# A feed-forward's first gate and value weights, split in the stage before it

## The chip, the cores and the metric

One NeuronCore of a Trainium2 chip. The time is the device's microseconds for one launch. TensorE multiplies matrices, VectorE and ScalarE do the elementwise work, GpSimd (POOL) small helpers and memsets, and the SP queue issues nearly all DMAs. All engines run by themselves and wait on semaphores.

## The reference

Two layers of a transformer trunk on 1024 tokens and 256 context tokens, width 1024. Each layer is a mixer (a convolution module and differential attention in layer 0, latent attention in layer 1), an output projection with norm, gate and residual, and a feed-forward. What matters here:

```python
def conv_ffn(h, w_up, conv_w, conv_b, w_down):
    u = h @ w_up
    val, gate = u[..., :FFN_HIDDEN], u[..., FFN_HIDDEN:]
    gate = depthwise_conv(gate, conv_w, conv_b)
    return (jax.nn.silu(gate) * val) @ w_down

x = x + mx[2] * rms_norm(yx, norm_mix_post[i])
hx = modulate(rms_norm(x, norm_ffn_pre[i]), mx[3], mx[4])
x = x + mx[5] * rms_norm(conv_ffn(hx, ...), norm_ffn_post[i])
```

`FFN_HIDDEN` is 2816, 22 tiles of 128. `w_up` is 1024 x 5632, the value half first.

## The kernel before

The kernel is a row of stages. Each has its own tiles in SBUF and its own semaphores; at its end the semaphores are cleared and all engines meet at a barrier (`stage`, L68, and `bare_stage`, L830; the barrier shows as L76). So no work of a stage begins before everything of the one before it is done.

**Exact products.** A float32 weight or activation is split into a rounded part, hi (type fp32r), and the rest, lo = raw - hi. `exact_product` (L84) takes three matmuls of 512 columns for one product: hi times hi, hi times lo, lo times hi (L88 to L90). Every weight must thus be loaded, rounded by ScalarE and subtracted by VectorE before TensorE may use it.

**The feed-forward** (`ffn`, L869; called twice: 10 token tiles in layer 0, 8 in layer 1). `raw`, `w_hi` and `w_lo` have four slots of 128 x 1024: value, gate and two for the down projection. One order of pieces, written by hand in `schedule`, is walked by every engine. It begins with the split of gate tile 0 (piece 0) and of value tile 0 (piece 1). A split is a 512 KB load on the SP queue (L977), a rounding on ScalarE (L1014) and a subtraction on VectorE (L1055) that raises `w_ready`. `product` on TensorE waits for `w_ready` at its piece and runs 8 x 3 matmuls for each chunk of up to 512 tokens. Behind piece 1 SP also loads the convolution's taps (L981, L983), and VectorE's `gate_work` waits for them, for the gate's chunks and for a memset of the sums by GpSimd (L1113). VectorE's first instruction in the stage is a memset of the gate tile (L1050), and bare increments follow it:

```python
dve.memset(gate[:, :], 0.0).then_inc(s.zeroed, 1)
dve.sem_inc(s.sum_done, SUMS)
```

**The join** (`join_project`, L1519) comes before the first feed-forward. It projects 10 token tiles with an output weight of 1024 x 1024, which it keeps split in `w_hi` and `w_lo` (8 slots of 1024 each). For tile t, behind TensorE's product: ScalarE copies and squares (L1747, L1753), GpSimd takes the inverse root (L1919, L1922), VectorE does the residual (L1859, L1863), ScalarE squares again (L1759), GpSimd takes a root, VectorE norms (L1868), TensorE turns (L1673), ScalarE modulates and rounds (L1769, L1774), VectorE subtracts (L1873). VectorE's order in loop step t is the residual of t-1, the norm of t-1, the rest of t-2. `work` has 8 slots of 1024: two for products, three for x, and others.

**The second output stage** (`project_out`, L1935) comes before the second feed-forward and does the same for 8 tiles with `TokenTail` (L246): VectorE runs `post_vector` of tile t (L344, L349), `pre_vector` of t-1 (L358, L362), `split_vector` of t-2 (L370, two halves). Its raw tile `y` has 8 slots; the weights' raw form lies in them at the start, and slots 0 and 1 take the products afterwards.

Of the kernel before, what the change touches and what calls it, by code (L numbers as in the profile page):

```python
# [11 lines left out]
ALU = mybir.AluOpType  # L12
# [856 lines left out]
def ffn(nc, name, tokens, h_hi, h_lo, y_sum, w_up, conv_w, conv_b, w_down, residual=None, following=None):  # L869
# [22 lines left out]
    with ExitStack() as ctx:  # L892
# [7 lines left out]
        w_hi = sb("w_hi", [P, 4, D], F32R)  # L900
        w_lo = sb("w_lo", [P, 4, D], F32R)
# [65 lines left out]
        def _(sp):  # L967
            def split(kind, tile, piece, back):
# [8 lines left out]
                sp.dma_start(raw[:, kind, :].rearrange("p (k n) -> p k n", n=src.shape[-1]), src)\  # L977
                  .then_inc(raw_in[kind], 16)
# [70 lines left out]
        def _(dve):  # L1049
# [3 lines left out]
            def split(kind, tile, piece, back):  # L1053
                dve.wait_ge(s.w_hi_done, piece + 1)
# [435 lines left out]
class OutWeights:  # L1490
# [3 lines left out]
    SIGNALS = ["w0_in", "w1_in", "w_hi_done", "w_ready"]  # L1494

    def __init__(self, nc, ctx, name, w_out, raw=None):
        self.w_out = w_out
        self.hi = ctx.enter_context(nc.sbuf_tensor(f"{name}_w_hi", [P, KD, D], F32R))
        self.lo = ctx.enter_context(nc.sbuf_tensor(f"{name}_w_lo", [P, KD, D], F32R))
        self.raw = raw if raw is not None else ctx.enter_context(nc.sbuf_tensor(f"{name}_raw", [P, 2, D], F32))  # L1500

    def load(self, sp, s, k):
        if k >= 2:

            sp.wait_ge(s.w_ready.sem, k - 1)
        sp.dma_start(self.raw[:, k % 2, :], self.w_out[k * P:(k + 1) * P, :])\
          .then_inc((s.w0_in, s.w1_in)[k % 2].sem, 16)

    def split_scalar(self, act, s, k):
        act.wait_ge((s.w0_in, s.w1_in)[k % 2].sem, 16 * (k // 2 + 1))  # L1510
        act.activation(self.hi[:, k, :], self.raw[:, k % 2, :], ACT.Copy).then_inc(s.w_hi_done.sem, 1)

    def split_vector(self, dve, s, k):
        dve.wait_ge(s.w_hi_done.sem, k + 1)
        dve.tensor_tensor(self.lo[:, k, :], self.raw[:, k % 2, :], self.hi[:, k, :].bitcast(F32), ALU.subtract)\
           .then_inc(s.w_ready.sem, 1)


def join_project(nc, y_hi, y_lo, conv_out, o_heads, ln_g, ln_b, subln, w_out, post, pre, x_old, x_new, ident):  # L1519
# [16 lines left out]
    with ExitStack() as ctx:  # L1536
        def sb(label, shape, dt=F32):
# [3 lines left out]
        w_hi, w_lo = (sb(f"w_{n}", [P, KD, D], F32R) for n in ("hi", "lo"))  # L1541
# [19 lines left out]
            "mean_full", "centred", "squared", "stat_full", "ms_done", "rstd_done", "spread", "normed", "silu_done",  # L1561
# [5 lines left out]
        block = ctx.enter_context(nc.Block())  # L1567

# [7 lines left out]
        def _(sp):  # L1576
# [56 lines left out]
        def _(pe):  # L1633
# [29 lines left out]
            def step(t, k, half):  # L1663
                cols_ = slice(half * BANK, (half + 1) * BANK)
                return exact_product(pe, ps[:, t % 2, cols_], y_hi[:, k, tokens(t)], y_lo[:, k, tokens(t)],
                                     w_hi[:, k, cols_], w_lo[:, k, cols_], k == 0, k == KD - 1)
# [47 lines left out]
        def _(act):  # L1714
            def weights(k):
                act.wait_ge(w_in[k].sem, 16)
                act.activation(w_hi[:, k, :], work[:, k, :], ACT.Copy).then_inc(s.w_hi_done.sem, 1)
# [82 lines left out]
        def _(dve):  # L1800
            def weights(k):
                dve.wait_ge(s.w_hi_done.sem, k + 1)
                dve.tensor_tensor(w_lo[:, k, :], work[:, k, :], w_hi[:, k, :].bitcast(F32), ALU.subtract)\
# [1320 lines left out]
```

## Time and profile before

| | us |
|---|---|
| median of 3 runs | 3630.87 |
| lowest and highest | 3623.41, 3631.25 |
| the profiled execution | 3627.79 |
| its span, first to last instruction | 3626.0 |
| TensorE busy | 3321.1 |
| VectorE busy | 1821.6 |
| ScalarE busy | 1169.1 |
| GpSimd busy | 294.6 |

The mean granted clock of TensorE was 0.956 of full speed. The execution's own time is 1.8 us over its span. Busy time is a mean over stages: in the feed-forwards TensorE is busy nearly all the time, at the stage boundaries no engine is. "<-" in a row names what released an engine from its idle time.

### The profile page before, as it was taken

Reading aid. Unit: us, or ns where it says so; the run is one execution under the profiler, and the core shown is the slowest. Engines: PE = TensorE matmul, PEld = TensorE weight load, DVE = VectorE, ACT = ScalarE, POOL = GpSimd, SP = SyncE. Lnnn points to the kernel's source line nnn. Section 1 sums busy time; section 2 is a strip of 40 time slices with the busy share of each in tenths; the row PEclk is TensorE's granted clock in tenths of the full one; section 3 lists DMA queues with packets and bytes.
Section 4 is the critical chain, followed back from the end, with each engine's and each line's share of the span. In section 5 each row is a group of like instructions: output and inputs, shape, how many; then the busy total and the mean of one; then the engine's idle time right before and its main releaser. Section 6 shows DMA issues by size and latency. Waiting matters only on the chain. (4 is left out here: it accounts for less than half of the span.)

```text
span 3626.0 us, 47627 instructions
## 1 busy us (share of the span) xinstructions
PE 3321.1 (92%) x18952; PEld 2782.4 (77%) x18952; DVE 1821.6 (50%) x2086; ACT 1169.1 (32%) x1913; POOL 294.6 (8%) x527
## 2 busy tenths in 40 slices
PE   3999599798999999999979698999999799999998
PEld 1787477676888888888869477888887688888886
DVE  4599666454344444444453334555554444444446
ACT  2212155456211111111146323555554322111121
POOL 1000000011000000000012111111111200000001
PEclk6999799889999999999989899999999899999999
DMA  5322587242211111111042743322212211111113
GB/s 182 83 83 97 160 276 240 102 127 76 63 50 40 35 35 35 35 40 41 30 135 83 260 167 97 103 51 53 60 40 76 73 62 48 51 46 58 35 47 116
DMA packets 277082, 316.29 MB, mean 87 GB/s; under 512 B 83825, under 2 KB 222673, under 8 KB 275905
## 3 DMA queue, kind: packets, MB, share of 16 engines
q1 hardware_dynamic: 264160, 267.09, 24.6%
q0 software_dynamic: 12768, 47.08, 3.5%
q8 instruction: 106, 1.74, 0.2%
q14 instruction: 48, 0.39, 0.0%
HBM read 243.54 MB, written 70.58 MB: 87 GB/s over the span
## 5 line engine op out<-in xcount | busy, mean ns | idle before, releaser
L1102 DVE TENSOR_TENSOR y_sum<-ffn_down_ps,y_sum 128x512 f32<-128x512 f32 x396 | 271.1, 690 | 238.2 <-PE ffn_down_ps L90 236.2
L88 PE MATMUL ffn_gate_ps<-y_hi,ffn_w_hi 128*128 128x512 f32 (+1 forms) x880 | 326.2, 371 | 22.6 <-DVE ffn_w_lo L1055 22.6
L88 PE MATMUL ffn_down_ps<-ffn_w_hi,ffn_act_hi 128*128 128x512 f32 x792 | 313.8, 396 | 16.8 <-DVE y_sum L1102 10.4
L89 PE MATMUL ffn_gate_ps<-y_lo,ffn_w_hi 128*128 128x512 f32 (+1 forms) x880 | 325.8, 370 | 0.0
L90 PE MATMUL ffn_gate_ps<-y_hi,ffn_w_lo 128*128 128x512 f32 (+1 forms) x880 | 325.6, 370 | 0.0
L89 PE MATMUL ffn_val_ps<-y_lo,ffn_w_hi 128*128 128x512 f32 (+1 forms) x880 | 323.9, 368 | 0.0
L88 PE MATMUL ffn_val_ps<-y_hi,ffn_w_hi 128*128 128x512 f32 (+1 forms) x880 | 323.8, 368 | 0.0
L90 PE MATMUL ffn_val_ps<-y_hi,ffn_w_lo 128*128 128x512 f32 (+1 forms) x880 | 323.7, 368 | 0.0
L89 PE MATMUL ffn_down_ps<-ffn_w_lo,ffn_act_hi 128*128 128x512 f32 x792 | 310.1, 392 | 0.0
L90 PE MATMUL ffn_down_ps<-ffn_w_hi,ffn_act_lo 128*128 128x512 f32 x792 | 309.8, 391 | 0.0
L1055 DVE TENSOR_TENSOR ffn_w_lo<-ffn_raw,ffn_w_hi 128x1024 fp32r<-128x1024 f32 x132 | 158.0, 1223 | 287.3 <-ACT ffn_w_hi L1014 287.3
L1035 ACT ACTIVATE ffn_act_hi<-ffn_conv 128x1024 fp32r<-128x1024 f32 x66 | 53.4, 841 | 593.3 <-DVE ffn_conv L1082 593.3
L2928 DVE TENSOR_REDUCE mla_neg_max<-mla_scores 128x1 f32<-128x1280 f32 x128 | 190.2, 1486 | 52.5 <-PE mla_scores L90 52.5
L1068 DVE TENSOR_SCALAR ffn_conv<-ffn_gate,ffn_taps 128x1281 f32<-128x1281 f32 (+1 forms) x44 | 38.8, 883 | 344.0 <-ACT ffn_gate L1024 344.0
L2842 PE MATMUL mla_turned<-ident,mla_e 128*128 128x128 f32 x1280 | 206.3, 275 | 1.9 <-ACT mla_pt L2906 1.3
L88 PEld LDWEIGHTS ffn_gate_ps<-y_hi,ffn_w_hi 128*128 128x128 f32 x880 | 167.2, 190 | 51.8 <-DVE ffn_w_lo L1055 23.4
L2898 ACT ACTIVATE mla_e<-mla_scores,mla_neg_max 128x1280 f32<-128x1280 f32 x128 | 170.0, 1328 | 111.6 <-DVE mla_neg_max L2928 111.6
L1014 ACT ACTIVATE ffn_w_hi<-ffn_raw 128x1024 fp32r<-128x1024 f32 x132 | 134.4, 1048 | 210.4 <-PE ffn_val_ps L90 195.5
L88 PEld LDWEIGHTS ffn_down_ps<-ffn_w_hi,ffn_act_hi 128*128 128x128 f32 x792 | 149.7, 189 | 59.2 <-DVE y_sum L1102 22.0
L2842 PEld LDWEIGHTS mla_turned<-ident,mla_e 128*128 128x128 f32 x1280 | 156.2, 141 | 48.0 <-issue 11.8
L666 DVE SCALAR_TENSOR_TENSOR ab_conv<-ab_u,ab_taps,ab_conv 128x1295 f32<-128x1295 f32 x120 | 188.1, 1567 | 3.2
L89 PEld LDWEIGHTS ffn_gate_ps<-y_lo,ffn_w_hi 128*128 128x128 f32 x880 | 167.2, 190 | 28.2
(293 smaller groups left out, 7022.9 us busy)
## 6 DMA issues: line engine op xcount, KB each, us to landing
ffn_raw<-in_ffn_w_up SPq DMA_DIRECT2D x88, 512.0 KB, 3.8
da_ada_w<-in_ada_w SPq DMA_DIRECT2D x10, 4096.0 KB, 24.5
ffn_raw<-in_ffn_w_down SPq DMA_DIRECT2D x44, 512.0 KB, 5.7
ab_raw<-in_ab_w_in SPq DMA_DIRECT2D x20, 512.0 KB, 3.8
mod_ada_w<-in_ada_w SPq DMA_DIRECT2D x4, 2048.0 KB, 11.1
scratch_mla_q_hi<-up_out_hi POOLq DMA_DIRECT2D x12, 512.0 KB, 2.9
scratch_mla_q_lo<-up_out_lo POOLq DMA_DIRECT2D x12, 512.0 KB, 3.2
scratch_qk_hi<-ab_qk_hi POOLq DMA_DIRECT2D x8, 640.0 KB, 3.2
```

Of the source, the lines that this page charges most:

```text
L88: pe.matmul(out, a_hi, b_hi, start=first, stop=False)
L89: pe.matmul(out, a_hi, b_lo, start=False, stop=False)
L90: return pe.matmul(out, a_lo, b_hi, start=False, stop=last)
L666: dve.scalar_tensor_tensor(out=out, in0=src[:, j:j + SPAN], scalar=taps[:, i, j:j + 1], in1=out, op0=ALU.mult, op1=ALU.add)\
L1014: act.activation(w_hi[:, kind, :], raw[:, kind, :], ACT.Copy).then_inc(s.w_hi_done, 1)
L1035: act.activation(act_hi[:, slot, b:b + m], conv[:, padded(b):padded(b) + m], ACT.Copy)\
L1055: dve.tensor_tensor(w_lo[:, kind, :], raw[:, kind, :], w_hi[:, kind, :].bitcast(F32), ALU.subtract).then_inc(s.w_ready, 1)
L1068: dve.tensor_scalar(inner, gate[:, 1:PAD - 1], here, bias, ALU.mult, ALU.add)\
L1102: dve.tensor_tensor(part, down_ps[:, half, :], part, ALU.add).then_inc(s.sum_done, 1)
L2842: mm = pe.transpose(t_ps[:, f % 2, m * P:(m + 1) * P], e[:, n % E_SLOTS, kt * P:(kt + 1) * P], ident[:, :])
L2898: act.activation(e[:, n % E_SLOTS, :], s_ps[:, n % 2, 0:T], ACT.Exp, bias=neg_max[:, n:n + 1], accum_out=sums[:, n:n + 1]).then_inc(s.exp. ...
L2928: dve.tensor_reduce(neg_max[:, n:n + 1], s_ps[:, n % 2, 0:T], AX.X, ALU.max, negate=True)\
```

## The change

The first gate tile and the first value tile of each feed-forward are loaded and split during the last tiles of the stage before it. The feed-forward's `w_hi` and `w_lo` become tiles that live across the boundary (`FirstWeights`, four slots each). While the output stage runs, these same tiles hold the upper half (k from 4 to 7) of that stage's own split weights (`Halves`); the lower half has tiles of its own. So the first split can be written only when TensorE has read the output weights for the last time, and VectorE waits for the last product (`y_full`). Both halves of the split, rounding and subtraction, are VectorE's now. In the feed-forward, pieces 0 and 1 are only increments.

```diff
+class FirstWeights:
+    SIGNALS = ["first0_in", "first1_in", "first_hi", "first_lo"]
+    KINDS = 1, 0
+    def __init__(self, nc, ctx, name, w_up, side):
+        self.hi, self.lo = (ctx.enter_context(nc.sbuf_tensor(f"{name}_first_{n}", [P, 4, D], F32R, side=side))
+                            for n in ("hi", "lo"))
+    def load(self, sp, n, raw, signal):
+        src = self.w_up.rearrange("(k p) (two f) -> p k two f", p=P, two=2)[:, :, self.KINDS[n], 0:P]
+        sp.dma_start(raw.rearrange("p (k n) -> p k n", n=P), src).then_inc(signal, 16)
+    def split(self, dve, n, raw, loaded, rounded, done):
+        kind = self.KINDS[n]
+        dve.wait_ge(loaded, 16)
+        dve.tensor_copy(self.hi[:, kind, :], raw).then_inc(rounded, 1)
+        dve.wait_ge(rounded, n + 1)
+        dve.tensor_tensor(self.lo[:, kind, :], raw, self.hi[:, kind, :].bitcast(F32), ALU.subtract).then_inc(done, 1)
+class Halves:
+    def at(self, k):
+        return self.lower[:, k, :] if k < KD // 2 else self.upper[:, k - KD // 2, :]
 def ffn(...)
-        w_hi = sb("w_hi", [P, 4, D], F32R)
-        w_lo = sb("w_lo", [P, 4, D], F32R)
+        w_hi, w_lo = first.hi, first.lo
   SP, split:
-                if not (isinstance(piece, int) and piece < 2):
+                if isinstance(piece, int) and piece < 2:
+                    sp.sem_inc(raw_in[kind], 16)
+                else:
                     sp.wait_ge(s.w_ready, piece - (back - 1))
...
   ScalarE, split:
+                if isinstance(piece, int) and piece < 2:
+                    act.sem_inc(s.w_hi_done, 1)
+                    return
   VectorE, split:
+                if isinstance(piece, int) and piece < 2:
+                    dve.sem_inc(s.w_ready, 1)
+                    return
 def join_project(...)
+        first_raw = [work[:, X + (N - 3) % 3, :], work[:, N % 2, :]]
   SP:
                 inputs(t + 2)
+                if t == N - 1:
+                    sp.wait_ge(x_stored[(N - 3) % 3].sem, 16 * ((N - 3) // 3 + 1))
+                    sp.wait_ge(s.h_done.sem, N - 2)
+                    first.load(sp, 0, first_raw[0], first_in[0])
                 store_x(t - 1)
+                if t == N - 1:
+                    first.load(sp, 1, first_raw[1], first_in[1])
   VectorE:
+                if t == N:
+                    dve.wait_ge(s.y_full.sem, N)
+                    first.split(dve, 0, first_raw[0], first_in[0], s.first_hi.sem, s.first_lo.sem)
                 if 1 <= t < N + 1:
                     residual(t - 1)
+                if t == N:
+                    first.split(dve, 1, first_raw[1], first_in[1], s.first_hi.sem, s.first_lo.sem)
 def project_out(...)
+        first, first_raw = weights.first, [y[:, 2, :], y[:, 3, :]]
   SP:
+                if t == N - 4:
+                    sp.wait_ge(s.w_ready.sem, KD)
+                    for n in range(2):
+                        first.load(sp, n, first_raw[n], first_in[n])
   VectorE:
+                if t == N - 1:
+                    dve.wait_ge(s.y_full.sem, N)
+                    first.split(dve, 0, first_raw[0], first_in[0], s.first_hi.sem, s.first_lo.sem)
                 if t < N:
                     tail.post_vector(dve, t, t, y[:, t % 2, :])
+                if t == N - 1:
+                    first.split(dve, 1, first_raw[1], first_in[1], s.first_hi.sem, s.first_lo.sem)
                 if 1 <= t < N + 1:
                     tail.pre_vector(dve, t - 1, t - 1)
```

Every use of the output weights changes from `w_hi[:, k, :]` to `w_hi.at(k)`, and likewise for lo.

## Rows read from the trace of the kernel before

**Rows 1.** The page, busy time, share of the span and instructions of each engine.

```profile
PE 3321.1 (92%) x18952; PEld 2782.4 (77%) x18952; DVE 1821.6 (50%) x2086; ACT 1169.1 (32%) x1913; POOL 294.6 (8%) x527
```

**Rows 2.** The chain that ended last, in order of time: start, duration, what.

```profile
2869.89 5.05 DMA ffn_raw<-in_ffn_w_up
...
2877.33 0.79 PE ffn_gate_ps L88
```

**Rows 3.** Timeline, first feed-forward's start: start us, duration us, engine, line, operation, [idle before].

```profile
903.25 1.22 DVE L1873 TENSOR_TENSOR y_lo<-out_work,y_hi 128x1024 fp32r<-128x1024 f32 x1 [4.12 <-ACT y_hi L1774]
...
905.50 8.63 POOL L1113 MEMSET y_sum<- 128x10240 f32 x1 [10.60 <-POOLq L76]
...
905.84 1.13 DVE L1050 MEMSET ffn_gate<- 128x1283 f32 x1 [1.36 <-PEq L76]
...
911.83 0.79 PE L88 MATMUL ffn_gate_ps<-y_hi,ffn_w_hi 128*128 128x512 f32 x1 [12.97 <-DVE ffn_w_lo L1055]
```

**Rows 4.** Timeline of VectorE, second feed-forward's start.

```profile
2868.36 0.69 DVE L370 TENSOR_TENSOR y_lo<-out_turned,y_hi 128x512 fp32r<-128x512 f32 x1 [0.16 <-ACT y_hi L406]
2870.17 0.91 DVE L1050 MEMSET ffn_gate<- 128x1026 f32 x1 [1.11 <-PEq L76]
```

**Rows 5.** Timeline of TensorE, first matmul of the latent attention.

```profile
2213.97 0.77 PE L88 MATMUL mla_scores<-k_first_hi,q_first_hi 96*128 96x512 f32 x1 [11.06 <-PEq L76]
```

**Rows 6.** Timeline of TensorE, where matmuls become short in each feed-forward.

```profile
917.12 0.42 PE L88 MATMUL ffn_gate_ps<-y_hi,ffn_w_hi 128*128 128x512 f32 x1
...
2883.04 0.49 PE L89 MATMUL ffn_gate_ps<-y_lo,ffn_w_hi 128*128 128x512 f32 x1
```

**Rows 7.** Groups of VectorE instructions, by form: count, busy us, mean ns, idle before.

```profile
L2936 DVE COPY mla_pt<-mla_turned 128x512 f32<-128x512 f32 x128 | 87.8, 686 | 131.7 <-PE mla_turned L2842 131.7
...
L1868 DVE TENSOR_SCALAR out_work<-out_work,out_small 128x1024 f32<-128x1024 f32 x10 | 7.5, 746 | 5.3 <-POOL out_small L1922 5.3
```

**Rows 8.** Timeline, the join's last tiles, VectorE, GpSimd and TensorE.

```profile
886.14 1.23 DVE L1873 TENSOR_TENSOR y_lo<-out_work,y_hi 128x1024 fp32r<-128x1024 f32 x1 [2.22 <-ACT y_hi L1774]
...
889.41 0.19 POOL L1919 TENSOR_SCALAR out_small<-out_small 128x1 f32<-128x1 f32 x1 [6.27 <-ACT out_work L1753]
889.68 0.55 POOL L1922 TENSOR_TENSOR out_small<-out_small,out_minus_half 128x1 f32<-128x1 f32 x1
...
890.26 1.28 DVE L1859 SCALAR_TENSOR_TENSOR out_work<-out_work,out_small,out_gates 128x1024 f32<-128x1024 f32 x1 [2.89 <-POOL out_small L1922]
...
894.93 0.75 DVE L1868 TENSOR_SCALAR out_work<-out_work,out_small 128x1024 f32<-128x1024 f32 x1 [2.13 <-POOL out_small L1922]
...
896.92 1.94 PE L1673 MATMUL out_turned<-ident,out_work 128*128 128x128 f32 x8 [8.97 <-ACT out_work L1769]
```

**Rows 9.** Timeline, the second output stage's last tiles.

```profile
2854.98 0.19 POOL L419 TENSOR_SCALAR out_small<-out_small 128x1 f32<-128x1 f32 x1 [7.97 <-ACT out_junk L389]
...
2857.15 1.22 DVE L349 TENSOR_TENSOR out_x<-out_x,out_raw 128x1024 f32<-128x1024 f32 x1
...
2857.25 1.53 POOL L421 TENSOR_TENSOR out_small<-out_small,out_minus_half 128x1 f32<-128x1 f32 x1
...
2858.82 1.28 DVE L358 SCALAR_TENSOR_TENSOR out_h<-out_x,out_small,out_rows 128x1024 f32<-128x1024 f32 x1 [0.44 <-POOL out_small L421]
```

**Rows 10.** The page, DMA issues: count, KB each, median us to landing.

```profile
ffn_raw<-in_ffn_w_up SPq DMA_DIRECT2D x88, 512.0 KB, 3.8
```

**Rows 11.** The taps in the first feed-forward: issue, landing, first use.

```profile
912.92 1.66 SPq L983 DMA_DIRECT2D ffn_taps<-in_ffn_conv_b  x1
...
ffn_taps<-in_ffn_conv_b SPq DMA_DIRECT2D x1, 11.0 KB, 5.1
...
928.80 0.95 DVE L1068 TENSOR_SCALAR ffn_conv<-ffn_gate,ffn_taps 128x1281 f32<-128x1281 f32 x1 [14.87 <-ACT ffn_gate L1024]
```

**Rows 12.** Timeline of TensorE, behind the first feed-forward's loop.

```profile
1802.48 0.77 PE L88 MATMUL ffn_down_ps<-ffn_w_hi,ffn_act_hi 128*128 128x512 f32 x1 [3.24 <-issue]
```

More of the change, by code:

```diff
@@ L866, in split_vector, with __init__, ffn @@
                           ALU.subtract).then_inc(s.next_ready, 1)
-def ffn(nc, name, tokens, h_hi, h_lo, y_sum, w_up, conv_w, conv_b, w_down, residual=None, following=None):
+class FirstWeights:
[4 more added lines that the diff above has]
+                            for n in ("hi", "lo"))
+        self.w_up = w_up
+    def load(self, sp, n, raw, signal):
[8 more added lines that the diff above has]
+class Halves:
+    def __init__(self, lower, upper):
+        self.lower, self.upper = lower, upper
+    def at(self, k):
+        return self.lower[:, k, :] if k < KD // 2 else self.upper[:, k - KD // 2, :]
+def ffn(nc, name, tokens, h_hi, h_lo, y_sum, w_up, conv_w, conv_b, w_down, first, residual=None, following=None):
     chunks = token_chunks(tokens)
@@ L972, in split @@
                     src = w_down[bass.ds(tile * P, P), :].rearrange("(k p) n -> p k n", k=1)
-                if not (isinstance(piece, int) and piece < 2):
+                if isinstance(piece, int) and piece < 2:
+                    sp.sem_inc(raw_in[kind], 16)
+                else:
                     sp.wait_ge(s.w_ready, piece - (back - 1))
                     sp.sem_inc(s.asked, 1)
-                sp.dma_start(raw[:, kind, :].rearrange("p (k n) -> p k n", n=src.shape[-1]), src)\
-                  .then_inc(raw_in[kind], 16)
+                    sp.dma_start(raw[:, kind, :].rearrange("p (k n) -> p k n", n=src.shape[-1]), src)\
+                      .then_inc(raw_in[kind], 16)
                 if isinstance(piece, int) and piece == 1:
@@ L1490, with __init__, join_project @@
 class OutWeights:
[L1494 to L1519, printed above, removed]
+    def __init__(self, nc, ctx, name, w_out, raw, first):
+        self.w_out, self.raw, self.first = w_out, raw, first
+        self.hi, self.lo = (Halves(ctx.enter_context(nc.sbuf_tensor(f"{name}_w_{n}", [P, KD // 2, D], F32R)), upper)
+                            for n, upper in (("hi", first.hi), ("lo", first.lo)))
+def join_project(nc, y_hi, y_lo, conv_out, o_heads, ln_g, ln_b, subln, w_out, post, pre, x_old, x_new, ident, first):
     AT = A_WIDTH // P
@@ L1540, in join_project @@
         work = sb("work", [P, 8, D])
-        w_hi, w_lo = (sb(f"w_{n}", [P, KD, D], F32R) for n in ("hi", "lo"))
+        w_hi, w_lo = (Halves(sb(f"w_{n}", [P, KD // 2, D], F32R), upper)
+                      for n, upper in (("hi", first.hi), ("lo", first.lo)))
         uo = sb("uo", [P, 2, KD, P])
@@ L1567, in join_project @@
         block = ctx.enter_context(nc.Block())
+        first_raw = [work[:, X + (N - 3) % 3, :], work[:, N % 2, :]]
+        first_in = [s.first0_in.sem, s.first1_in.sem]
         def tokens(t):
@@ L1942, in project_out @@
         ps = ctx.enter_context(nc.psum_tensor(f"{name}_ps", [P, 2, D], F32))
-        s = ctx.enter_context(stage(nc, name, TokenTail.SIGNALS + ["y_full", "y_copied", "w_hi_done", "w_ready"]))
+        s = ctx.enter_context(stage(nc, name, TokenTail.SIGNALS + ["y_full", "y_copied", "w_hi_done", "w_ready"]
+                                    + FirstWeights.SIGNALS))
+        first, first_raw = weights.first, [y[:, 2, :], y[:, 3, :]]
+        first_in = [s.first0_in.sem, s.first1_in.sem]
         tail = TokenTail(nc, ctx, name, s, post, pre, 2 if tokens > SEQ else 1, N, ident)
@@ L3077, in trunk @@
                 first_head.close()
-                weights = OutWeights(nc, projection, "out1", i.c_w_out[0], w_raw)
+                first = FirstWeights(nc, layer1, "ffn1", i.ffn_w_up[1], "right")
+                weights = OutWeights(nc, projection, "out1", i.c_w_out[0], w_raw, first)
                 project_out(nc, "out1", y_hi, y_lo, SEQ, weights, (mods(1, MIX_GATE, 1), i.norm_mix_post[1]),
@@ L3083, in trunk @@
                 ffn(nc, "ffn1", SEQ, y_hi, y_lo, y_sum, i.ffn_w_up[1], i.ffn_conv_w[1], i.ffn_conv_b[1],
-                    i.ffn_w_down[1], ((mods(1, FFN_GATE, 1), i.norm_ffn_post[1]), tile_of(x3), tile_of(out)))
+                    i.ffn_w_down[1], first, ((mods(1, FFN_GATE, 1), i.norm_ffn_post[1]), tile_of(x3), tile_of(out)))
 def rope_constants():
```

23 lines of the change are left out of this document (13 added, 10 removed).

## The prediction

> **What bounds the kernel now.** I read the page's busy times first: TensorE is busy for 3321.1 of 3626.0 us [rows 1], so only what makes TensorE wait, or runs it at its lower clock, is worth anything. Then the chain that ended last, in order of time: it runs through the second feed-forward and begins with that stage's first weights, a DMA at 2869.89, ScalarE's rounding, VectorE's subtraction and TensorE's first matmul at 2877.33 [rows 2]. That is 7.44 us in which nothing but these weights is on its way. Last, the timeline at both stage boundaries. In the first feed-forward the join's last operation ends at 904.47 (903.25 + 1.22), GpSimd starts the next stage at 905.50, VectorE its memset at 905.84, and TensorE gets its first weights at 911.83 after 12.97 us of idling [rows 3]. In the second the end of the stage before is 2869.05 (2868.36 + 0.69), VectorE starts at 2870.17 [rows 4] and TensorE at 2877.33 [rows 2]. From each first matmul on, TensorE sets the time, so an earlier start moves the rest by as much.
>
> **What the change removes.** At each feed-forward's start: two loads of 512 KB, two roundings, two subtractions; the engines raise the semaphores instead. TensorE then waits for one thing, VectorE's increment of w_ready, which stands in VectorE's queue behind the memset of the gate tile. Two bounds. If the increment goes as soon as the memset is under way, TensorE starts a little after 905.84. If it goes only when the memset has ended, TensorE starts just after 906.97 (905.84 + 1.13). The kernel has no row for such a bare increment with an engine waiting for it. But where a bare increment must follow an operation (lines 2624 and 2625), the code puts a wait before it, so I take the earlier side, with some time for the semaphore: 906.25. The first feed-forward gains 911.83 - 906.25 = 5.6 us (4.8 at the other bound, 5.9 at most). TensorE can start this soon after a boundary: the latent attention, which waits for nothing, has its first matmul at 2213.97 straight behind the barrier [rows 5].
>
> **The clock.** TensorE starts each feed-forward at the lower level (1.2 GHz): its matmuls of 512 columns become short (0.42 us and less) only at 917.12, 5.3 us after the start, and in the second at 2883.04, 5.7 us after it [rows 6]. The last turn of the join, at 896.92, already takes 1.94 us for 8 small matmuls [rows 8] and is followed by a pause either way. The shorter pause (7.4 us instead of 13.0) gives me no reason for a warm start, so this cold piece moves and stays. It costs nothing here; for the range, half a cold piece more or less is about 1.3 us each (half of 5.3, at half speed).
>
> **What it adds: a copy and a subtraction on VectorE, twice per boundary.** The subtraction has the form of the one at 903.25, 1.22 us [rows 3]. A VectorE copy from SBUF to SBUF of 1024 is not in the trace. Below it stands the one-source operation of that size, 0.75 us (L1868); above, the copy of 512 from PSUM takes 0.69 us, so 1024 at that rate is under 1.4 us [rows 7]. It has one source in SBUF, like L1868, so I take 0.75; with 0.04 between, one split is 2.02 us, at most 2.65.
> The Trainium skill (VectorE: DVE Perf Modes, section on the perf-mode tier table) puts an fp32 tensor_copy and tensor_scalar in SBUF in one class at double rate; by that rule it is 0.75 too. I have no run of the copy.
>
> **First boundary, gate split.** It sits behind the wait for the last product and before the residual of tile 9. TensorE's last product ends at 886.92 (896.92 less 8.97 idle less the 1.03 of the turn behind it); VectorE is free at 887.37 (886.14 + 1.23). So the split runs 887.40 to 889.42 (to 890.05 at most). GpSimd starts the root at 889.41 and VectorE takes it up at 890.26 [rows 8]: the idle time covers the split. What it can cost is the delay of GpSimd's operation, 0 to 0.7 us; I take 0.1. A delay here is on the path, since the residual feeds ScalarE, which does tile 8's modulation next.
> **Value split.** Behind the residual, 892.85 to 894.87. The norm of tile 9 stood at 894.93, released by GpSimd [rows 8], whose two steps now fall beside the subtraction. The second stage shows what that does: GpSimd's root takes 0.55 us alone [rows 8], but 1.53 (2857.25 to 2858.78) beside a VectorE addition that ends at 2858.37 [rows 9]. So the norm starts at about 895.6 and ends at 896.35. The turn that reads it starts at 896.92, and waits for ScalarE [rows 8]: 0.5 us to spare, cost nothing; with the slow copy the spare is used up and up to 0.3 us shows.
> The Trainium skill (GPSIMD Engine Reference, Specifications) says GpSimd shares its SBUF interfaces with VectorE when VectorE reads two SBUF inputs or runs in a 2-port mode. This speaks against both splits, whose copy is in the second class and subtraction in the first; the sum by it is the one just made, since the 1.53 us row already has it.
>
> **Second boundary, gate split.** In the first stage GpSimd's root started 2.5 us behind the product's end, so here (2854.98) the product ends near 2852.5 and the split is over near 2854.6: covered, 0 to 0.6 us, and I take 0.
> **Value split.** Here there is no cover. VectorE ends the residual at 2858.37, waits 0.45 us, and from 2858.82 works almost without a pause through tiles 6 and 7: each one's scaling, shift and the subtractions between [rows 9]; the turns and roundings follow these. The split of 2.02 and its gap go in at 2858.40, so 2858.82 becomes 2860.47. All behind it goes 1.65 us later, and so does the stage's end (2.3 at most by the slow copy; 0.4 more if GpSimd's root of 2857.25 has to wait out the split as well). TensorE starts the second feed-forward at 2870.17 + 1.65 + 0.4 = 2872.2. It gains 2877.33 - 2872.2 = 5.1 us. With the increment behind the memset (0.91) it gains 4.55.
>
> **Queues.** In SP's queue of the join the gate load waits for tile 7's store and norm, both older than the store of tile 8 behind it, so nothing is held up. Each raw tile is queued a product ahead of its split; such a load lands in 3.8 us [rows 10]. In the feed-forward the taps' four small loads are now first in SP's queue. The last was issued at 912.92 and landed 5.1 us later, at 918.0; they come 1.06 us sooner, so at 917.0. VectorE needed them at 928.80 and will at 923.2 [rows 11]: 6 us to spare, and in the second stage some 3. GpSimd's memset of the sums, also awaited there, ends at 914.13 (905.50 + 8.63) [rows 3]. Later tiles' loads and TensorE's loop are untouched.
>
> **The sum.** 5.6 - 0.1 + 5.1 = 10.6 us. The profiled execution took 3627.79 us (span 3626.0), which gives 3617.2. The shown median, 3630.87, is 3.1 higher, the lowest run 4.4 lower; all four executions average 3628.3, less 10.6 is 3617.7. I say 3618.
>
> **Rivals.**
> (a) The increment waits for the memset and the copy is slow: 4.8 - 0.8 + 4.55 - 0.65 = 7.9 us, 3620. For it: both bounds above are open. Against: the copy has the shape of L1868. This is the weak end of the same case.
> (b) TensorE's instructions are not there at the boundary. After the loop, at 1802.48, it sat idle for 3.24 us with nothing that the trace shows to wait for [rows 12]. If that came behind each barrier, TensorE would start near 908.8 (905.5 + 3.24) and 2874.8: 3.0 + 2.5 - 0.1 = 5.4 us, 3623. Against: rows 5, and both boundaries are straight code.
> (c) Slower. A second wait, now hidden behind the weights, ends at 911.83 and 7 us behind the second barrier (the same 3.24 twice over, or a late barrier), so no start is gained. The value split's 1.65 to 2.7 us on the second boundary and the gate split's 0.1 to 0.7 remain: 1.8 to 3.4 us slower, 3630 to 3631. It decides once that hidden wait ends later than 6.3 us behind the barrier. Against: TensorE followed VectorE's subtraction at once in both places.
> (d) The clock comes back sooner in the second stage, since the turns lie only 3 us ahead of the first product: up to 2.8 us more gain, 3615. For it: the shorter pause. Against: the turns there run cold and are few.
>
> **Chances.** Forecast with (a) as its end 0.78, (b) 0.07, (c) 0.04, (d) 0.11. The range adds the clock's 1.3 us twice, (a), and the runs' own scatter of about 4 us either way: 3612 to 3625. A change under 0.2% (7.3 us) can't be told from none here. By the median shown, faster means below 3623.6. I give faster 0.80, within 0.2% 0.17, slower 0.03.
>
> **What would show it.** First matmul of the first feed-forward near 906.3 and 5.4 us after it the fast matmuls. In the join, the residual of tile 9 at 890.3 or 890.4, the norm near 895.6, the last subtraction still at 903.3. In the second stage tile 6's scaling 1.65 us later than now against the residual before it, and the stage's end as much. No VectorE wait on the taps. The copy at 0.75 us. I am wrong if TensorE idles over 2 us behind a barrier, if the turn at 896.92 moves by more than 0.5 us, or if the second boundary's gain is under 4.

## The result, and the profile after

The changed kernel takes 3636.18 us (median of 20 runs, 3627.09 to 3643.13), the kernel before, on the same chip, 3625.23 (median of 20 runs, 3618.03 to 3634.78): ratio 1.0028, 95% interval 1.0022 to 1.0035. It is slower by 0.3%, where I had forecast 3618 and 0.3% faster, and it lies outside my range of 3612 to 3625.

The profiled execution took 3635.7 us, its span is 3633.9 and the mean granted clock 0.958 (before: 3627.79, 3626.0, 0.956). So the clock is no cause of the loss. The page's busy times, to be held against [rows 1]:

```profile
PE 3343.7 (92%) x18952; PEld 2783.4 (77%) x18952; DVE 1824.0 (50%) x2090; ACT 1164.2 (32%) x1909; POOL 294.8 (8%) x527
```

TensorE executes the same 18952 matmuls and is busy for 22.6 us more. VectorE has the 4 operations more and ScalarE the 4 fewer that the diff says. So I looked for the lost time inside TensorE's own work, not in a wait.

Both boundaries, on the other hand, did what was forecast. The timeline of the changed kernel (columns as in [rows 3]), first the join's last tiles and the first feed-forward's start, then the second output stage's and the second feed-forward's start:

```profile
886.40 0.69 DVE L888 CAST ffn_first_hi<-out_work 128x1024 fp32r<-128x1024 f32 x1
887.12 1.23 DVE L890 TENSOR_TENSOR ffn_first_lo<-out_work,ffn_first_hi 128x1024 fp32r<-128x1024 f32 x1
888.54 0.19 POOL L1957 TENSOR_SCALAR out_small<-out_small 128x1 f32<-128x1 f32 x1 [6.28 <-ACT out_work L1786]
...
889.39 1.28 DVE L1892 SCALAR_TENSOR_TENSOR out_work<-out_work,out_small,out_gates 128x1024 f32<-128x1024 f32 x1 [1.04 <-POOL out_small L1960]
...
892.57 1.23 DVE L890 TENSOR_TENSOR ffn_first_lo<-out_work,ffn_first_hi 128x1024 fp32r<-128x1024 f32 x1
893.21 0.64 POOL L1957 TENSOR_SCALAR out_small<-out_small 128x1 f32<-128x1 f32 x1 [3.85 <-ACT out_work L1792]
...
894.51 0.75 DVE L1901 TENSOR_SCALAR out_work<-out_work,out_small 128x1024 f32<-128x1024 f32 x1 [0.71 <-POOL out_small L1960]
...
902.37 1.23 DVE L1906 TENSOR_TENSOR y_lo<-out_work,y_hi 128x1024 fp32r<-128x1024 f32 x1 [4.11 <-ACT y_hi L1807]
904.65 8.64 POOL L1153 MEMSET y_sum<- 128x10240 f32 x1 [10.17 <-POOLq L76]
...
904.87 0.80 PE L88 MATMUL ffn_gate_ps<-y_hi,ffn_first_hi 128*128 128x512 f32 x1 [6.88 <-DVEq L1092]
904.99 1.13 DVE L1087 MEMSET ffn_gate<- 128x1283 f32 x1 [1.39 <-PEq L76]
...
2849.24 1.23 DVE L349 TENSOR_TENSOR out_x<-out_x,out_raw 128x1024 f32<-128x1024 f32 x1
2849.34 1.76 POOL L421 TENSOR_TENSOR out_small<-out_small,out_minus_half 128x1 f32<-128x1 f32 x1
2850.39 0.68 DVE L888 CAST ffn_first_hi<-out_raw 128x1024 fp32r<-128x1024 f32 x1
...
2852.25 1.28 DVE L358 SCALAR_TENSOR_TENSOR out_h<-out_x,out_small,out_rows 128x1024 f32<-128x1024 f32 x1
...
2861.78 0.69 DVE L370 TENSOR_TENSOR y_lo<-out_turned,y_hi 128x512 fp32r<-128x512 f32 x1 [0.16 <-ACT y_hi L406]
...
2863.56 0.79 PE L88 MATMUL ffn_gate_ps<-y_hi,ffn_first_hi 128*128 128x512 f32 x1 [2.44 <-DVEq L1092]
2863.62 0.91 DVE L1087 MEMSET ffn_gate<- 128x1026 f32 x1 [1.14 <-PEq L76]
```

This trace runs 0.88 us ahead of the one before already at the join's last tiles (902.37 against 903.25 [rows 3]). At the first boundary TensorE starts 1.27 us behind the end of the stage (903.60 to 904.87), where it started 7.36 behind it. At the second it starts 1.09 us behind (2862.47 to 2863.56), where it was 8.28. The second feed-forward starts at 2863.56 instead of 2877.33, 13.8 us sooner, and yet the span ends 7.9 us later. So its 748.7 us have become 770.3.

That stage can be read off one row. ScalarE rounds each of the 22 hidden tiles once, just behind TensorE's products for it. The view of that tile's instructions (count, shortest, median and longest in ns, start of the first and of the last), second feed-forward, kernel before:

```profile
L1035 ACT ACTIVATE ffn_act_hi<-ffn_conv x22: 1056/1061/1064, 2905.8 to 3584.3; 128x1024 fp32r<-128x1024 f32 x22
```

the first feed-forward (44 instructions) in the kernel before and in the changed one, and the changed kernel's second:

```profile
L1035 ACT ACTIVATE ffn_act_hi<-ffn_conv x44: 397/729/1062, 946.1 to 1800.7; 128x1024 fp32r<-128x1024 f32 x22, 128x256 fp32r<-128x256 f32 x22
...
L1072 ACT ACTIVATE ffn_act_hi<-ffn_conv x44: 397/729/1062, 938.8 to 1793.4; 128x1024 fp32r<-128x1024 f32 x22, 128x256 fp32r<-128x256 f32 x22
...
L1072 ACT ACTIVATE ffn_act_hi<-ffn_conv x22: 1056/1060/1062, 2892.3 to 3590.9; 128x1024 fp32r<-128x1024 f32 x22
```

From first to last tile the second feed-forward takes 698.6 us instead of 678.5. The first takes 854.6, and 854.6 before. Below I call this the tile time. The distance from one 512-column matmul's start to the next (mean over some 250 to 400 neighbours, in windows spread over the stage), which I call the step, tells the same:

```
step, ns                     gate    value   down   | output stage ahead
before, 1st feed-forward     226.9   227.3   227.3  | 228.8
before, 2nd                  226.7   226.6   227.4  | 227.1
changed, 1st                 226.9   227.3   227.3  | 228.8
changed, 2nd                 234.2   234.3   233.4  | 232.2
```

The granted clock is 1.00 in both kernels from 2910 to 3560 us. The second feed-forward has 3168 such matmuls, and 3168 at 7 ns more are 22 us: that is the loss. What differs between the two feed-forwards is where the diff put their tiles. The tiles' addresses, which no trace shows, are, in bytes along a partition: before, w_hi and w_lo of the second at 100992 and 117376; changed, first_lo at 196576 and first_hi at 212960, since they were allocated on the right side of the memory, which is filled from 229344 downwards. The first feed-forward's went to 100992 and 117376. I give addresses by what is left over a multiple of 256: y_hi, y_lo and the activations stand at 128 in both kernels, so do all feed-forward weights of before and the changed kernel's first ring (the four slots of first_hi and first_lo), but the second ring stands at 224.

### The profile page after: what moved, and what is told of

Same layout as the page of the kernel before. It is cut to its first block and busy times, and to the rows that moved or that the text cites. A ratio compares the mean times of both kernels' runs of the same rounds, so it can differ in the third digit from the quotient of the medians.

```text
span 3633.9 us, 47642 instructions
## 1 busy us (share of the span) xinstructions
PE 3343.7 (92%) x18952; PEld 2783.4 (77%) x18952; DVE 1824.0 (50%) x2090; ACT 1164.2 (32%) x1909; POOL 294.8 (8%) x527
## 3 DMA queue, kind: packets, MB, share of 16 engines
q1 hardware_dynamic: 264160, 267.09, 24.6%
## 5 line engine op out<-in xcount | busy, mean ns | idle before, releaser
L88 PE MATMUL ffn_gate_ps<-y_hi,ffn_first_hi 128*128 128x512 f32 (+1 forms) x880 | 328.6, 373 | 9.3 <-DVEq L1092 9.3
L88 PE MATMUL ffn_down_ps<-ffn_first_hi,ffn_act_hi 128*128 128x512 f32 x792 | 315.2, 398 | 15.7 <-DVE y_sum L1142 9.2
L89 PE MATMUL ffn_gate_ps<-y_lo,ffn_first_hi 128*128 128x512 f32 (+1 forms) x880 | 328.2, 373 | 0.0
L90 PE MATMUL ffn_gate_ps<-y_hi,ffn_first_lo 128*128 128x512 f32 (+1 forms) x880 | 327.9, 373 | 0.0
L89 PE MATMUL ffn_val_ps<-y_lo,ffn_first_hi 128*128 128x512 f32 (+1 forms) x880 | 326.7, 371 | 0.0
L88 PE MATMUL ffn_val_ps<-y_hi,ffn_first_hi 128*128 128x512 f32 (+1 forms) x880 | 326.5, 371 | 0.0
L90 PE MATMUL ffn_val_ps<-y_hi,ffn_first_lo 128*128 128x512 f32 (+1 forms) x880 | 326.3, 371 | 0.0
L90 PE MATMUL ffn_down_ps<-ffn_first_hi,ffn_act_lo 128*128 128x512 f32 x792 | 311.7, 394 | 0.0
L89 PE MATMUL ffn_down_ps<-ffn_first_lo,ffn_act_hi 128*128 128x512 f32 x792 | 311.0, 393 | 0.0
L88 PEld LDWEIGHTS ffn_gate_ps<-y_hi,ffn_first_hi 128*128 128x128 f32 x880 | 167.4, 190 | 40.7 <-DVEq L1092 10.1
L88 PEld LDWEIGHTS ffn_down_ps<-ffn_first_hi,ffn_act_hi 128*128 128x128 f32 x792 | 149.4, 189 | 59.5 <-DVE y_sum L1142 20.9
L89 PEld LDWEIGHTS ffn_gate_ps<-y_lo,ffn_first_hi 128*128 128x128 f32 x880 | 167.3, 190 | 30.4
L90 PEld LDWEIGHTS ffn_gate_ps<-y_hi,ffn_first_lo 128*128 128x128 f32 x880 | 167.2, 190 | 30.5
```

Of the source, the lines that this page charges most:

```text
L88: pe.matmul(out, a_hi, b_hi, start=first, stop=False)
L89: pe.matmul(out, a_hi, b_lo, start=False, stop=False)
L90: return pe.matmul(out, a_lo, b_hi, start=False, stop=last)
```

## The experiments

My theory from here on: the start address of a matmul's operand costs TensorE time. Rivals: the ring as such (two stages sharing tiles, the upper half used by the output stage), or the loads and splits that are missing at the stage's start. For each run I give the time and, as ratio or difference, how it stands to the kernel before on the same chip; where there is a single run, I say so and go by its trace.

**Ring moved by 32 bytes (e1), weights of before moved by 32 bytes and its activations by 64 (e2), only the first boundary changed (e3), second boundary with the gate weights alone (e4).**

```
e1: + layer1.enter_context(nc.sbuf_tensor("pad1", [P, 8], F32, side="right"))
      first = FirstWeights(nc, layer1, "ffn1", i.ffn_w_up[1], "right")
e2: + if name == "ffn1": sb("pad_a", [P, 8])      # ahead of w_hi
    + if name == "ffn1": sb("pad_b", [P, 8])      # behind w_lo
e3: - first = FirstWeights(nc, layer1, "ffn1", i.ffn_w_up[1], "right")
    + first = None       # output weights and the stage's start as before
e4: e1, and
    + EARLY = 1 if name == "ffn1" else 2          # pieces that are split ahead
    - first.split(dve, 1, first_raw[1], ...)      # value split of project_out
```

> The kernel after, with 32 bytes of padding on the right side of SBUF ahead of the second feed-forward's early weights, so that they begin at multiples of 64 bytes (196544 and 212928 instead of 196576 and 212960). Theory A (a matrix operand that begins 32 bytes past a multiple of 64 makes every matmul step slower): the chunks of the second feed-forward come back from 5.62 to 5.44 us, the output stage's tile from 12.02 to 11.79, and the kernel is about 22 + 2 us faster than the kernel after, so some 14 to 16 us faster than the kernel before (ratio 0.996). Theory B (the weights lie too far up in SBUF, beside the sums): no change by 32 bytes, ratio stays 1.003. Theory C (something else in the second stage's new order): also 1.003.

> The kernel before, with 32 bytes of padding ahead of the second feed-forward's w_hi and w_lo and 32 bytes behind them; only these two tiles move (101024 and 117408 instead of 100992 and 117376), nothing of the early split is in it. Theory A: chunks of 5.62 us in the second feed-forward alone, about 22 us slower, ratio 1.006. Theories B and C: as before, ratio 1.000.

> The early split at the first boundary only; the second output stage and feed-forward as in the kernel before. All theories: the first boundary's gain alone, about 6.4 us (ratio 0.998), and no slow chunks in the second feed-forward. If the first boundary's gain were lost later, the ratio would be 1.000.

> The padded kernel, and at the second boundary only the gate tile is split early; the value tile is loaded, rounded and subtracted inside the feed-forward as before, beside the gate product. Expected if the value split's 1.3 us on VectorE's path is what the output stage's end gained in length: 1.3 us less than the padded kernel, TensorE's first value product not delayed. With theory A true the ratio to the kernel before is 0.995 to 0.996; with B or C 1.002 to 1.003.

Measured: e1 3627.01 us, 1.0008 (0.9999 to 1.0017), steps 233.3, 233.2 and, down, 229.0: a multiple of 64 gave back only part, so neither of my forecasts for e1 (0.996 or 1.003) came. e2 3641.69 us, 1.0051 (1.0037 to 1.0065), steps 233.3 in all three. e3 3616.32 us, 0.9979 (0.9969 to 0.9988), steps 227. e4 3625.89 us, 1.0004 (0.9995 to 1.0013), steps as e1.

e2 is the decisive one: the kernel before, with its stages untouched and some tiles of its second feed-forward further up, loses nearly what the changed kernel loses there. The two pads move more than its expectation says: the weights go from 128 to 160 over a multiple of 256, and the activations, which lie behind both pads, to 192. Its tile time is 697.0 us:

```profile
L1039 ACT ACTIVATE ffn_act_hi<-ffn_conv x22: 1056/1060/1062, 2901.0 to 3598.0; 128x1024 fp32r<-128x1024 f32 x22
```

So the loss comes without the ring and with all splits in their old place; e8 and e16 below show the other side, a ring without the loss. e3 shows the first boundary's gain alone. e4 shows no gain from the value split at the second boundary: the stage's end comes 1.3 us sooner without it (10.68 us behind the residual, 12.01 in e1), and e4 and e1 can't be told apart in time.

**Other operands, other distances (e5, e6, e7), ring moved by 96 bytes (e8).**

```
e5: kernel before; pads of 8 floats ahead of y_hi1 and of act_hi (second
    feed-forward), weights not to be moved off their multiples of 128
e6: w_hi, w_lo = (sb(n, [P, 4 * D + 32], F32R)[:, at:at + 4 * D]...)
    # at = 4 floats in the first feed-forward, 12 in the second
e7: the same with at = 24 and 16
e8: e1 with [P, 24] in place of [P, 8]
```

> The kernel before, with the other matmul operands of the second output stage and feed-forward moved: y_hi1 and y_lo1 begin at 19104 and 51872 (32 past a multiple of 128), the two act tiles likewise; the weights stay at multiples of 128. So the gate and value products have a shifted moving operand only, the down product and the output product a shifted stationary one only. Steps so far (start to start, 512 columns): 227 ns with all tiles at multiples of 128; 233.3 with the weights at 32 past, in either role. Theory A1 (the start of either operand counts, whichever tile it is): 233 ns in all three products and in the output product. Theory A2 (it is something of the weight tiles alone): 227.

> The kernel before, with w_hi and w_lo of the first feed-forward beginning 16 bytes past a multiple of 128, and of the second 48 past. Theory A (every start off the grid costs the same): 233 ns in both feed-forwards. If only multiples of 32 other than 0 cost: 227 in the first. If the cost grows with the offset, the second is slower than the first.

> The kernel before, with w_hi and w_lo of the first feed-forward beginning 96 bytes past a multiple of 128 and of the second 64 past, low in SBUF. The kernel after had 96 past and lay high: 234.2 ns for gate and value (weights stationary), 233.4 for down (weights moving). The padded one had 64 past and lay high: 233.3 and 229.0. Theory A with a grid of 128 bytes: the same pairs here, 234.2 and 233.4 in the first feed-forward, 233.3 and 229.0 in the second. Theory B2 (a grid of 64, and the high place costs the rest): 233 in the first, 227 and 227 in the second.

> The kernel after, with 96 bytes of padding in place of 32 ahead of the second feed-forward's early weights: they begin at 196480 and 212864, multiples of 128, as high up as before. Grid of 128: 227 ns in every product, the kernel some 14 us faster than before (ratio 0.996). Theory B2 (the high place): 233 and 229 as in the first padded kernel, ratio 1.001.

Measured: e5 3643.07 us, a single run, steps 234.3 (gate, value), 233.3 (down), 233.4 (output). e6 3649.46, a single run, first feed-forward 234.3, 234.5 and 231.3, second 230.1, 229.8 and 232.0. e7 3658.09, a single run, first 233.0, 232.9 and 233.3, second 231.7, 231.9 and 230.5. e8 3609.37 us, 0.9958 (0.9944 to 0.9971), all steps of the second feed-forward 226.6 to 227.0.

e8 gives back all of it, and beats both kernels. From these runs I concluded that every operand had to start on a multiple of 128. That was wrong, and two slips hid it: in e5 the pads took the weights from 128 to 0 over a multiple of 256 (y to 160, the activations to 32), and in e6 and e7 the tiles had grown by 128 bytes, so that w_lo stood 128 off w_hi. The steps of e6 and e7 fit none of the rules written down for them.

**All other matmul tiles on multiples of 128 (e9), the same with the gate weights alone (e10), and 128 bytes or one tile alone (e11).**

```
e9:  e8, its 96 bytes now at the top of the right side (the latent
     attention's q and k move too), + sb("pad", [P, 24]) ahead of lat_h_hi
e10: e9, and e4's edit
e11: kernel before; at = 32, 32 floats (w_hi, w_lo) in the first
     feed-forward, 0, 8 in the second, in tiles that grew by 128 bytes
```

> The kernel after with 96 bytes of padding at the top of SBUF's right side, once, so that every tile on that side begins at a multiple of 128 (the second feed-forward's early weights at 196480 and 212864, and the latent attention's first head's q and k too, which were 96 past in the kernel before), and 96 bytes ahead of the latents stage's h_hi and h_lo, which were 32 past in the kernel before. Theory: the ratio of the kernel padded to 128 (0.996) and, if the latents' moving tiles paid as the weights did, up to 240 x 3 matmuls x 5 ns = 3.6 us more, about 0.995. If short matmuls and another bound hide it there: 0.996.

> The kernel with all tiles on the grid of 128, and the value split of the second boundary left in the feed-forward. The value split lengthened VectorE's path from the last residual to the stage's end from 10.68 to 12.01 us; here 10.68, so 1.3 us less than the kernel with all on the grid; below what the rounds can tell (0.1%), so the trace decides.

> The kernel before, with w_hi and w_lo of the first feed-forward 128 bytes further on (multiples of 256, where every fast case so far was 128 past one), and in the second only w_lo moved, to 32 past a multiple of 128. If the grid is 128: 227 ns in the first feed-forward. If it matters which half of 256 a tile begins in: slower. If each instruction pays for its own operand: in the second feed-forward one matmul in three (the one that reads w_lo) pays 6.5 ns, a mean of 229; if one shifted tile slows the whole row: 233.

Measured: e9 3609.5 us, 0.9960 (0.9946 to 0.9974), e10 3608.46, 0.9961 (0.9948 to 0.9975): nothing more to gain there, and again no difference by the value split. e11 3648.45 us, a single run, 24.6 over the kernel before: in the first feed-forward the gate and value steps are 233.1 and 233.2, down 228.9, although every tile starts on a multiple of 128. (w_hi stood at 0 over a multiple of 256 and w_lo, for the grown tile, at 128.) In the second, where w_lo came to 32 over a multiple of 256, they are 233.3, 233.4 and, down, 231.8. My rule fell. Nearly all tiles of the kernel before stand at 128 over a multiple of 256, so place by itself and place against the other operand had never been told apart.

**Everything moved alike (e12, e13), one operand by 128 bytes, one tile by 32 (e14, e15).**

```
e12: + sb("pad_all", [P, 8])     # ahead of the first tile: all 32 bytes up
e13: + sb("pad_all", [P, 32])    # all 128 bytes up
e14: w tiles grown by 256 bytes; first: both at 32 floats; second: 0 and 8
e15: the same; first: act tiles at 32 floats, w at 0; second: w_hi 8, w_lo 0
```

> The kernel before with one pad of 32 bytes ahead of its first tile, so that nearly every tile of it (weights, hidden rows, activations, alike) starts 32 bytes further up and all stand as before to each other: all at 160 over a multiple of 256, where before all stood at 128. Nothing else changes. Theory A (what counts is where an operand starts by itself, and the good place is the one that all tiles of before share): both feed-forwards and the output stages step 6 to 8 ns longer per 512-column product (227 to 233 or more), some 6700 of them in the two feed-forwards and more elsewhere, so the time is 45 to 60 us over the kernel before. Theory B (what counts is how the stationary and the moving operand of one product stand to each other): every step stays at 226.6 to 227.4 ns and the time stays within 3 us of the kernel before.

> The kernel before with a pad of 128 bytes ahead of its first tile: nearly all tiles start at a multiple of 256 where before they stood 128 over one. Theory A with a grid of 128 bytes: no change, steps of 227 ns. Theory A with a grid of 256 (which the last look suggests, where the first feed-forward's w_hi stood at a multiple of 256 and stepped 233 ns): steps of 233 ns, time 45 us up or more. Theory B: steps of 227 ns and the time of the kernel before, within 3 us.

> The kernel before with the feed-forwards' weights in views of larger tiles. First feed-forward: w_hi and w_lo both start 128 bytes further up (multiples of 256), the hidden rows and activations stay at 128 over one. Second: w_hi stays, w_lo alone starts 32 bytes further up. A grid of 128: the first feed-forward stays at 227 ns. A grid of 256, by itself or between the two operands: 230 to 234 ns in gate, value and down products. If only the relation of hi to lo counts, the first stays at 227 ns, since both moved alike. Second: if a shifted tile costs only the products that read it, the value and gate steps rise by a third of the full 7 ns (one product of three reads w_lo), to 229 ns; if one shifted tile disturbs its neighbours in the order too, to 233 ns as with both shifted.

> The kernel before with weights and activations of the feed-forwards in views of larger tiles. First feed-forward: activations start 128 bytes further up (a multiple of 256), weights stay: gate and value products stay at 227 ns by every theory (if they don't, the distance of the tiles w_hi and w_lo, now 16640 bytes instead of 16384, counts), and the down products, with act stationary at 0 and weights moving at 128 over a multiple of 256, stay at 227 ns with a grid of 128 and go to 229 to 234 ns with one of 256. Second: w_hi alone starts 32 bytes further up: two of three products read it, so 231 to 232 ns if only those pay, 233 ns or more if the third pays too.

Measured, a single run each, kernel before 3627.06: e12 3628.57 and e13 3627.09, every step within 0.3 ns of before. e14 3665.18: first feed-forward 232.6, 232.4 and 232.3, second 233.5, 233.4 and 232.3. e15 3651.11: first 227.2, 227.4 and down 232.2, second 231.8, 231.8 and 232.5. The tile times of the second feed-forward, e12:

```profile
L1035 ACT ACTIVATE ffn_act_hi<-ffn_conv x22: 1056/1061/1064, 2905.2 to 3583.7; 128x1024 fp32r<-128x1024 f32 x22
```

678.5 us to the tenth as before, with nearly all tiles at 160, where e2 had the weights at 160, y at 128 and the activations at 192 and paid 18.5 us. So 160 is not a bad place by itself, nor is 128 needed (e13 has nearly all at 0); what counts is how the two operands of a product stand to each other. e14's first feed-forward (871.2 us of tile time against 854.6) shows that 128 bytes between them cost, too. In e15's first, w_lo stands 256 bytes further from y than in before, and gate and value are at 227: 256 cost nothing.

**The changed kernel's ring left where it is, the rest brought to it (e16).**

```
e16: changed kernel, + sb("pad_all", [P, 24])   # left side 96 bytes up: to 224
```

> The changed kernel with its ring of first weights left where it is (196576 and 212960, 224 over a multiple of 256), and one pad of 96 bytes ahead of the first tile on the left side, so that hidden rows, y, the output stages' lower halves and the activations come to 224 over a multiple of 256 too. By the relation of the two operands (what the last four looks showed for the kernel before) the second feed-forward steps at 227 ns again, the last output stage too, and the time is that of the version with the ring moved: 0.9945 to 0.9970 of the kernel before. By a place that is good or bad in itself, it keeps the 234 ns in the second feed-forward: 1.002 to 1.004, or worse still where the first one joins it.

Measured: 3610.88 us, 0.9967 (0.9952 to 0.9981), steps 226.7, 226.7 and 227.1, output stage 227.1, and the tile time 678.3:

```profile
L1072 ACT ACTIVATE ffn_act_hi<-ffn_conv x22: 1056/1062/1064, 2890.6 to 3568.9; 128x1024 fp32r<-128x1024 f32 x22
```

The ring is at 196576 and 212960 as in the changed kernel, and the loss is gone. The feed-forward products in which hi and lo stood alike, and e5's output stage, by the stationary operand's start less the moving one's, modulo 256:

```
difference   step, ns         where
  0          226.6 to 227.4   before, e8, e9, e10, e12, e13, e16
 32          233.3            e2 gate, value, down; e5 down
 64          233.2, 233.3     e1 gate, value
 96          234.2 to 234.3   changed kernel and e5, gate and value
128          232.2 to 232.6   e14 first feed-forward; e15 first, down
160          233.4            changed kernel, down; e5 output stage
192          229.0            e1 down
```

**One tile alone: where the cost falls.** In e14's second feed-forward only w_lo is off. The timeline of TensorE there, matmuls and, last, the weight load (PEld) of an L90:

```profile
3000.07 0.40 PE L88 MATMUL ffn_gate_ps<-y_hi,ffn_w_hi 128*128 128x512 f32 x1
3000.31 0.40 PE L89 MATMUL ffn_gate_ps<-y_lo,ffn_w_hi 128*128 128x512 f32 x1
3000.55 0.39 PE L90 MATMUL ffn_gate_ps<-y_hi,ffn_w_lo 128*128 128x512 f32 x1
3000.78 0.40 PE L88 MATMUL ffn_gate_ps<-y_hi,ffn_w_hi 128*128 128x512 f32 x1
...
3000.31 0.19 PEld L90 LDWEIGHTS ffn_gate_ps<-y_hi,ffn_w_lo 128*128 128x128 f32 x1
```

The product with w_lo is L90. Over the some 700 gate and value steps of each line in that stage, the one that begins with L89 is the long one, 239.0 ns; the one that begins with L90 itself is 228.3, and L88's 232.6 (before: 226.6 to 226.8). While L89 streams y_lo, the weights of L90 are being loaded. So most of the cost falls in the product during which the misplaced tile is loaded, and little in the one that multiplies by it. It is not all of it: L88's step neither reads nor loads w_lo and is 5.9 ns longer too. In e15's second feed-forward, with w_hi alone off, all three are longer: L88 231.7, L89 230.8 (during which w_lo, in its old place, is loaded), L90 233.1. The loads' own mean stays at 187 to 188 ns in every kernel, so the trace shows the moving operand delayed, not the load. That the two reads collide in the memory is my reading of this; no run shows it directly, and a collision of these two reads alone doesn't explain L88's step.

## Why the prediction was wrong

**The step that failed** is "Later tiles' loads and TensorE's loop are untouched", and with it "From each first matmul on, TensorE sets the time, so an earlier start moves the rest by as much". The diff moves the loop's weights to other addresses, and I never asked what that does to 3168 matmuls. It held because of a premise at the very start, "only what makes TensorE wait, or runs it at its lower clock, is worth anything": TensorE's rate at full clock was taken as fixed, and it is not. The misplaced operands cost 21.7 us in the second feed-forward and about 1.8 in the output stage ahead of it, whose upper weight halves are the same tiles (its tiles' turns are 12.02 us apart, 11.79 before). None of my rivals had it; my slower one, (c), was a hidden wait, and no such wait appeared. None of the signs of being wrong that I had named came either (TensorE starts 1.3 and 1.1 us behind the two stages' ends, the turn of 896.92 keeps its place, the second boundary gains 5.9 us): they all looked at the boundaries, and the loss was in the stage behind.

**The rest held.** With the two operands brought together the kernel takes 3609.37 us (e8), 13.9 under the kernel before on its chip, where I had 10.6; e9, e10 and e16 are 14.3, 15.4 and 12.8 under theirs. The interval of e8 is 10.5 to 20.3 us, so my sum was at its low end. Part of the rest is the clock, as shown below, and not a better start.

- First boundary: 6.1 us from the earlier start, 5.6 forecast. The bare increment didn't wait for the memset: TensorE's matmul at 904.87 is earlier than the memset's start at 904.99. The cold piece, up to the first short matmul, is 4.4 us (904.87 to 909.31) instead of 5.3 (917.12 less 911.83 [rows 3, 6]), so the gain is 6.4 by the first hidden tile (938.8 against 946.1, less the 0.9 of lead).
- Copy: 0.69 us, 0.75 forecast; subtraction 1.23.
- Gate split in the join: GpSimd starts at 888.54, which is 889.41 [rows 8] less the 0.88 by which this trace is ahead, and the residual at 889.39, 890.26 [rows 8] less the same: cost nothing, 0.1 forecast.
- Value split there: GpSimd's first step took 0.64 us instead of 0.19 beside the subtraction, and the norm came at 894.51, 0.46 us late against 894.93 [rows 8] (0.7 forecast). The last subtraction kept its place: 902.37. The Trainium skill (GPSIMD Engine Reference, Specifications) names two-input VectorE instructions as contenders for the interfaces that GpSimd shares; these rows agree.
- Second boundary: the value split costs 1.32 us (12.00 from the residual's end to the stage's, 10.68 before [rows 4, 9]), 1.65 forecast. The 0.45 us in which VectorE waited for GpSimd vanished into it, though GpSimd's root stretched to 1.76 us. TensorE's start against the residual's end gained 5.9 us (18.96 [rows 2, 9] to 13.09), 5.1 forecast.
- Rival (d), a warmer start, came in small: cold pieces of 4.4 us and, in the second (2863.56 to 2868.42), 4.9, for 5.3 and 5.7. It is not one number: at the first boundary the traces have 4.0 to 5.7 us where the weights are loaded behind the barrier, and 3.2 to 4.9 where they are ready. Rival (b)'s 3.24 us [rows 12] did not come behind the barriers.
- Taps: no VectorE wait on them; its first operation on the gate, at 921.51, was released by ScalarE.

The account by the two traces: 0.9 us ahead at the join, 6.4 at the first boundary, 5.9 at the second, and 0.6 in between (some 2.4 gained, less the output stage's 1.8) make the 13.8 us by which the second feed-forward starts sooner; its own 21.7 turn them into 7.9 lost. The 2.4 are the clock's. Behind the first feed-forward's loop TensorE pauses in both kernels, for 3.24 us [rows 12] and 3.25. Then the kernel before executes 12 matmuls at the lower level, 0.63 us or more each, and the changed kernel none; first the kernel before, then the changed one:

```profile
1803.05 0.63 PE L89 MATMUL ffn_down_ps<-ffn_w_lo,ffn_act_hi 128*128 128x512 f32 x1
...
1795.17 0.47 PE L88 MATMUL ffn_down_ps<-ffn_first_hi,ffn_act_hi 128*128 128x512 f32 x1 [3.25 <-issue]
1795.48 0.39 PE L89 MATMUL ffn_down_ps<-ffn_first_lo,ffn_act_hi 128*128 128x512 f32 x1
```

The lead grows from 7.3 us ahead of these matmuls to 9.8 behind them, and what the clock gives and takes in the stages after that nearly cancels. I don't count this as a gain of the early split: e7, which splits at the old place, has no such slow matmuls either, and e8, which splits early, has 8.

## What to carry to other kernels

When a change moves a tile that TensorE reads, note the start address, and compare stationary and moving operand modulo 256 bytes: a pad of 24 floats (96 bytes) was worth 0.6 to 0.7% of this kernel, more than the change itself. Where a change takes waits away and the time still grows, look at the busy engine's own rate first (one row per stage, first and last start at equal counts) before looking for a new wait. And when a placement rule seems found, move everything by the same amount once: here that told a place that is bad from two places that don't match.

## What was not expected of the hardware

- TensorE's 512-column products in this kernel's fp32r step at 226.6 to 227.4 ns when the two operands start alike modulo 256 bytes, and at 229.0 to 234.3 ns when they don't, by up to 3.3%, with the granted clock the same. In the second feed-forwards compared here that clock was 1.00. The Trainium skill (SBUF — State Buffer, Operand start alignment) states where an operand may start and says that its runs timed nothing; these do.
- The cost is not monotonic in the distance: 192 costs 2 ns, 96 costs 7.5. Of 64 and 96 only gate and value products were seen (stationary weights), of 192 only down products (moving weights). A distance of 224 was not tried, nor one that is no multiple of 32 with both tiles alike, nor other operand types. Why it is 256 stays open.
- A tile that is out of place slows products that don't read it: with w_lo alone off, the steps of the two products of w_hi were 232.6 and 239.0 ns (e14); in e15 with w_hi alone off that of the product of w_lo was 233.1.
